# A hybrid decoder layer on one core: gate strips together, branch strips together, recurrent gates one tile later

## What is computed

```
xn = rmsnorm(x) * norm_mix
xl, gl, q, k, v, z, b, a, u_pool, g_lru, g_dn, g_pool = split(xn @ w_in)
o_lru  = rg_lru(conv4(xl)) * gelu(gl)          # gates: tanh of block-diagonal products of conv4(xl)
o_dn   = gated_delta_rule(silu(conv4(q,k,v)), b, a) ... * silu(z)
o_pool = multiscale causal pooling of u_pool
merged = sigmoid(g_lru)*(o_lru @ w_br_lru) + sigmoid(g_dn)*(o_dn @ w_br_dn) + sigmoid(g_pool)*(o_pool @ w_br_pool)
x = x + merged @ w_out
x = x + relu(rmsnorm(x) @ w_up)**2 @ w_down
y = rmsnorm(x) * norm_final
```

## Time and profile before

| what | value |
|---|---|
| time, median of 3 runs | 2197.82 us (2196.42 to 2201.01) |
| profiled execution, its own time | 2197.58 us |
| its span | 2195.8 us |
| PE busy (matmul) | 2157.2 us, 98% |
| DVE, ACT, POOL busy | 1223.4, 784.4, 176.0 us |
| DMA mean | 141 GB/s |

### The profile page before, as it was taken

One profiled execution on the slowest core, in us unless ns is written; L12 is line 12 of the kernel. 1 busy time (PEld: TensorE's weight loads), 2 busy tenths in 40 slices (PEclk: granted clock), 3 DMA queues, 4 the chain that ended last, 5 costly groups with the idle time before them and its releaser, 6 DMA issues.

```text
span 2195.8 us, 35754 instructions
## 1 busy us (share of the span) xinstructions
PE 2157.2 (98%) x14507; PEld 2096.5 (95%) x14507; DVE 1223.4 (56%) x1993; ACT 784.4 (36%) x946; POOL 176.0 (8%) x325
## 2 busy tenths in 40 slices
PE   8999998999999999999999999999999999999997
PEld 8998997899998899989999999999999999999997
DVE  7996786555566555555554554444444444444444
ACT  5434553222222222233333443333333333333243
POOL 7000011110022110010000100000000000000001
PEclk9999999999999999999999999999999999999998
DMA  6454444343354343346444444444444544444443
GB/s 216 140 158 135 130 126 132 107 121 113 96 171 125 107 122 109 96 136 197 149 146 153 151 143 149 150 153 146 152 148 150 153 146 149 153 148 153 145 144 106
DMA packets 295610, 308.96 MB, mean 141 GB/s; under 512 B 9713, under 2 KB 290417, under 8 KB 295233
## 3 DMA queue, kind: packets, MB, share of 16 engines
q1 hardware_dynamic: 291616, 291.54, 43.0%
q0 software_dynamic: 3584, 15.55, 2.4%
q10 hardware_dynamic: 288, 0.15, 0.0%
HBM read 298.83 MB, written 8.37 MB: 140 GB/s over the span
## 4 chain that ended last, share of the span: by engine, by line
PE 85%; DVE 8%; ACT 3%; issue 3%; POOL 1%; DMA 1%; DVEq 0%; ACTq 0%; SPq 0%; POOLq 0%
PE main L1420 26%; PE main L1421 25%; PE main L1422 25%; PE aux L1540 6%; DVE scratch L883 2%; DVE scratch L876 2%; DVE lo L876 1%; ACT hi L608 1%; DMA raw<-in_w_in 1%; DVE scratch L880 1%; PE aux L1523 0%; PE aux L1513 0%; POOL qkv L368 0%; DVE merged L876 0%; DVE scratch L879 0%
## 5 line engine op out<-in xcount | busy, mean ns | idle before, releaser
L876 DVE TENSOR_TENSOR lo<-raw,hi 128x1024 fp32r<-128x1024 f32 x546 | 670.0, 1235 | 571.6 <-ACT hi L608 565.4
L608 ACT ACTIVATE hi<-raw 128x1024 fp32r<-128x1024 f32 x546 | 573.4, 1056 | 934.8 <-PE main L1422 920.2
L1420 PE MATMUL main<-x_hi,hi 128*128 128x320 f32 x2688 | 842.8, 314 | 3.0 <-DVE x_lo L883 1.7
L1421 PE MATMUL main<-x_lo,hi 128*128 128x320 f32 x2688 | 831.6, 309 | 0.0
L1422 PE MATMUL main<-x_hi,lo 128*128 128x320 f32 x2688 | 831.5, 309 | 0.0
L1420 PEld LDWEIGHTS main<-x_hi,hi 128*128 128x128 f32 x2688 | 505.9, 188 | 10.5 <-issue 5.2
L1421 PEld LDWEIGHTS main<-x_lo,hi 128*128 128x128 f32 x2688 | 506.0, 188 | 0.8 <-issue 0.2
L1422 PEld LDWEIGHTS main<-x_hi,lo 128*128 128x128 f32 x2688 | 505.5, 188 | 0.0
L1420 PE MATMUL main<-o_hi,hi 128*128 128x320 f32 x1408 | 442.4, 314 | 4.6 <-DVE o_lo L876 4.6
L1421 PE MATMUL main<-o_lo,hi 128*128 128x320 f32 x1408 | 435.5, 309 | 0.0
L1422 PE MATMUL main<-o_hi,lo 128*128 128x320 f32 x1408 | 435.5, 309 | 0.0
(11 more groups left out here) (249 smaller groups left out, 1187.7 us busy)
## 6 DMA issues: line engine op xcount, KB each, us to landing
raw<-in_w_in SPq DMA_DIRECT2D x210, 512.0 KB, 3.7
raw<-in_w_up SPq DMA_DIRECT2D x128, 512.0 KB, 3.8
raw<-in_w_down SPq DMA_DIRECT2D x128, 512.0 KB, 3.4
raw<-in_w_back SPq DMA_DIRECT2D x80, 512.0 KB, 3.4
scratch<-in_s_in POOLq DMA_DIRECT2D x8, 512.0 KB, 4.7
out_s_out<-scratch POOLq DMA_DIRECT2D x8, 512.0 KB, 4.5
merged<-in_x SPq DMA_DIRECT2D x8, 320.0 KB, 7.7
qkv<-in_x POOLq DMA_DIRECT2D x1, 2560.0 KB, 10.4
```

The costliest lines, as they stand in the source:

```text
L608: act.activation(HI[:, slot * TILE:(slot + 1) * TILE], RAW[:, slot * TILE:(slot + 1) * TILE], ACT.Copy).then_inc(hi_ready, 1)
L876: return dve.tensor_tensor(out, a, b, op)
L1420: pe.matmul(bank, hi, xh, start=first, stop=False)
L1421: pe.matmul(bank, hi, xl, start=False, stop=False)
```

## The change

A gated iteration runs both gate strips (tiles 0 to 7), then both branch strips (tiles 8 to 11), with loads in the same new order. There are two gate buffers, `GATE = (GS, GS1)`. The memory of the second comes from `RN` and `BG`, which become halves of `GS`. On DVE `gate(1)` stands at position 12 (was: position 2 of the next iteration), `merge(0)` at position 2 of the next iteration (was: position 10), and ACT's tanh goes with the gate. The products `gates(it)` of the LRU pass, which stood at the end of tile 7, stand at the end of tile 0 of the next iteration, or of the first tile of `GPL`. PE's loop over the LRU iterations is unrolled. DVE's and ACT's orders in the LRU pass are as they were.

```diff
-        GS = sb("gate", 2 * N)
-        RN, BG = sb("qk_scale_rows", N), sb("beta_gamma_rows", N)
+        GS, GS1 = sb("gate", 2 * N), sb("gate_second", 2 * N)
+        GATE = (GS, GS1)
+        RN, BG = GS[:, 0:N], GS[:, N:2 * N]
...
             def gated(it, n0, name):
                 for s in range(2):
                     for j in range(4):
-                        load(n0, 12, it, 6 * s + j, A["w_in"], j * 512, it * 512 + (G0[name] + s * 256))
+                        load(n0, 12, it, 4 * s + j, A["w_in"], j * 512, it * 512 + (G0[name] + s * 256))
+                for s in range(2):
                     for j in range(2):
-                        load(n0, 12, it, 6 * s + 4 + j, A["w_back"], BACK[name] + j * 512, it * 512 + s * 256)
+                        load(n0, 12, it, 8 + 2 * s + j, A["w_back"], BACK[name] + j * 512, it * 512 + s * 256)
...
-                own = {8: [lambda: gate(it, 0, t0, 0)]}
+                own = {8: [lambda: gate(it, 0, t0, 0)], 12: [lambda: gate(it, 1, t0, 0)]}
...
             def gate(n0, t0, it, s):
-                tile_done(n0, 12, it, 6 * s + 3)
-                dve.wait_ge(evacuated, it * 8 + (t0 + 4 * s + RING))
-                for m in range(2):
-                    tt(GS[:, m * N:(m + 1) * N], MB[m][:, 0:N], R[:], ALU.mult).then_inc(evacuated, 1)
+                tile_done(n0, 12, it, 4 * s + 3)
+                dve.wait_ge(evacuated, it * 8 + (t0 + 2 * s + RING))
+                for m in range(2):
+                    tt(GATE[s][:, m * N:(m + 1) * N], MB[2 * s + m][:, 0:N], R[:], ALU.mult).then_inc(evacuated, 1)
...
-                own = {8: [lambda: gate(n0, t0, it, 0)], 10: [lambda: merge(n0, t0, g0, it, 0, branch)]}
+                own = {8: [lambda: gate(n0, t0, it, 0)], 12: [lambda: gate(n0, t0, it, 1)]}
...
-                steps = {2: [lambda: gate(n0, t0, it, 1)], 4: [lambda: merge(n0, t0, g0, it, 1, branch)]}
+                steps = {2: [lambda: merge(n0, t0, g0, it, 0, branch)], 4: [lambda: merge(n0, t0, g0, it, 1, branch)]}
...
-                    3: [(7, lambda: qk_sums(3))], 7: [(7, lambda: gates(0))]})
-            with pe.Fori(1, 4) as it:
-                lru(it, {7: [(7, lambda: gates(it))]})
+                    3: [(7, lambda: qk_sums(3))]})
+            for it in range(1, 4):
+                lru(it, {0: [(7, lambda it=it: gates(it - 1))]})
...
-                    strip(n0, 12, t0, 8, it, 6 * s, 4 * s, XH, XL, between=between)
-
-                    strip(n0, 12, t0, 8, it, 6 * s + 4, 4 * s + 2, OH, OL,
+                    strip(n0, 12, t0, 8, it, 4 * s, 2 * s, XH, XL, between=between)
+                for s in range(2):
+                    strip(n0, 12, t0, 8, it, 2 * s + 8, 2 * s + 4, OH, OL,
...
-            gated(0, GPL_N, GPL_T, 0, 4, 0)
+            gated(0, GPL_N, GPL_T, 0, 4, 0, {0: [(7, lambda: gates(3))]})
```

More of the change, by code:

```diff
@@ L727, in gate @@
             def gate(it, s, t0, g0):
-                act.wait_ge(evacuated, it * 8 + (t0 + 4 * s + 2 + RING))
-                act.activation(GS[:], GS[:], ACT.Tanh, scale=0.5).then_inc(gate_ready, 1)
+                act.wait_ge(evacuated, it * 8 + (t0 + 2 * s + 2 + RING))
+                act.activation(GATE[s][:], GATE[s][:], ACT.Tanh, scale=0.5).then_inc(gate_ready, 1)
             def dn_step(h, k):
@@ L766, in late @@
             def late(it, t0, h0):
-                steps = {2: [lambda: gate(it, 1, t0, 0)]}
-                return steps if h0 is None else joined(steps, dn_steps(dn_step, it + h0, False, True))
+                return dn_steps(dn_step, it + h0, False, True)
             gated(0, GPL_N, GPL_T, 0, lru_steps(lru_step, 3), True)
@@ L803, in gated_dn @@
                 walk(split, GPD_N, 12, it, 12, {**after, 8: [lambda: gate(it, 0, GPD_T, 0)],
-                                                10: [lambda: merged_hi(it * 2)]})
+                                                12: [lambda: gate(it, 1, GPD_T, 0)]})
             def late_dn(it):
-                return {2: [lambda: gate(it, 1, GPD_T, 0)], 4: [lambda: merged_hi(it * 2 + 1)]}
+                return {2: [lambda: merged_hi(it * 2)], 4: [lambda: merged_hi(it * 2 + 1)]}
             gated_dn(0, {4: [lambda: z_gate(3)]})
@@ L1055, in row_norms @@
                 dve.wait_ge(sq_used, 1 + 16)
-                link(rsqrt(2, AX[1][0:16, 0:N], ROW[4], ROW[5], ROW[6], RN[0:16, :], 1.0, SMALL[0:16, 0:1]))
+                link(rsqrt(2, AX[1][0:16, 0:N], ROW[4], ROW[5], ROW[6], RN[0:16], 1.0, SMALL[0:16, 0:1]))
                 rows_split(0, RN)
@@ L1121, in gate @@
             def gate(n0, t0, it, s):
-                tile_done(n0, 12, it, 6 * s + 3)
-                dve.wait_ge(evacuated, it * 8 + (t0 + 4 * s + RING))
+                tile_done(n0, 12, it, 4 * s + 3)
+                dve.wait_ge(evacuated, it * 8 + (t0 + 2 * s + RING))
                 for m in range(2):
-                    tt(GS[:, m * N:(m + 1) * N], MB[m][:, 0:N], R[:], ALU.mult).then_inc(evacuated, 1)
+                    tt(GATE[s][:, m * N:(m + 1) * N], MB[2 * s + m][:, 0:N], R[:], ALU.mult).then_inc(evacuated, 1)
             def merge(n0, t0, g0, it, s, branch):
-                tile_done(n0, 12, it, 6 * s + 5)
+                tile_done(n0, 12, it, 2 * s + 9)
                 dve.wait_ge(gate_ready, it * 2 + (g0 + s + 1))
                 for m in range(2):
-                    dst = GS[:, m * N:(m + 1) * N] if branch else cols(MG, it, 4 * N, (2 * s + m) * N, N)
-                    stt(dst, GS[:, m * N:(m + 1) * N], 1.0, MB[2 + m][:, 0:N], ALU.add, ALU.mult) \
+                    own = GATE[s][:, m * N:(m + 1) * N]
+                    dst = own if branch else cols(MG, it, 4 * N, (2 * s + m) * N, N)
+                    stt(dst, own, 1.0, MB[2 * s + m][:, 0:N], ALU.add, ALU.mult) \
                         .then_inc(evacuated, 1)
@@ L1136, in merge @@
                     return
-                dve.wait_ge(evacuated, it * 8 + (t0 + 4 * s + 4 + RING))
+                dve.wait_ge(evacuated, it * 8 + (t0 + 2 * s + 6 + RING))
                 sums = cols(MG, it, 4 * N, 2 * s * N, 2 * N)
-                ins = tt(sums, sums, GS[:], ALU.add)
+                ins = tt(sums, sums, GATE[s][:], ALU.add)
                 if branch == 1:
```

## The result

| | before | changed |
|---|---|---|
| median of the runs | 2198.4 us (4 runs, 2196.4 to 2201.0) | 2212.3 us (4 runs, 2210.9 to 2214.9) |
| ratio, 95% interval | | 1.0066 (1.0050 to 1.0082) |
| profiled execution, own time | 2197.6 us | 2212.4 us |
| its span | 2195.8 us | 2210.6 us |
| granted clock, mean | 0.994 | 0.992 |

The changed kernel is slower by some 14 us. PE's work is the same, as the page's line of busy time shows against the earlier trace rows: 3 us more on 14507 instructions, which is slow clock, since the instructions are the same.

What follows compares the result with a forecast made beforehand. PE is busy 98%, but the LRU pass was taken as bound by a closed chain through PE, ACT and DVE. 8.0 + 4.8 + 4.3 + 1.4 + 0.3 = +18.8 on 2197.6 gave 2216.4, as median 2216.6 us, range 2206 to 2224.

Steps and rivals of the forecast that it cites:

- The chain in the LRU pass: LRU pass: the convolution comes 2.65 us later in each of three periods, 34.5 instead of 31.9; +8.0 us.
- The head of `GPL`: Head of `GPL`: ACT's tanh, `o_ready` and the first head's step 0 come 4.8 us later, without cover; +4.8 us.
- The clock in front of step 0: Tile 0 in two looped LRU iterations and at `GPL`'s head: new PE waits lower the clock; +4.3 us.
- The clock behind step 0: Behind the first head's step 0 in `GPL`: clock low after PE's wait of 9 to 10 us; +1.4 us.
- The moved gates and merges: Gated passes: changed DVE orders, gains at merges against losses at the gate; +0.3 us, from -2.6 to +5.
- The scaling ahead of step 9: Position 12 in each of two passes: strip 1's gate delays the head's steps; +0.88 us each, +1.8.
- The merge that left the place ahead of step 1: First iteration of `GPL`: gain of up to 0.88 us, half usable, -0.4; in `GPP` -1.1.
- The looped iterations: Looped gated iterations: costed at nothing, covered by a half tile of 1.8 us; otherwise up to 0.9 each of six.
- the second buffer frees PE: Rival: gate products hide behind tile 0, PE's waits and a slow stretch go; -9.9, 2187.7 us; chance 7%.
- The balance: Rival: half the chain's growth hidden, clock stays up, losses met by a removed wait; about 2198 us; chance 4%.
- The case without the clock: Rival: the chain grows but the clock stays high; 13.1 us slower, 2211 us; chance 15%.
- The case where the clock costs more: Rival: a second slow stretch follows each slow tile 0, doubling both clock terms; 2222 us; chance 12%.

Runs made afterwards that it cites:

- e5: The changed kernel with DVE's convolution one position later, behind the split of the next tile 0 instead of ahead of it: 2199.7 us, ratio 1.0007.
- e3: The changed kernel with POOL's rows of the first head computed ahead of its wait for `o_ready`: 2207.9 us, ratio 1.0040.
- e4: e1 with POOL's rows of the first head computed ahead of its wait for `o_ready`: 2193.6 us, ratio 0.9982.
- e6: The changed kernel plus 16 unused matmuls at the end of tile 7 in the last three LRU iterations: 2208.8 us, ratio 1.0052.
- e2: The kernel before with only the gate products moved behind tile 0, gated passes and their one buffer kept: 2211.2 us, ratio 1.0059.
- e1: The kernel before with only the new gated order and two gate buffers, gate products still at tile 7: 2196.8 us, ratio 0.9995.
- e10: e4 with gate strip 1's scaling and tanh moved into the next iteration, and three ACT splits ahead of LRU steps in `GPL`: 2189.8 us.
- e8: e1 with the scaling of gate strip 1 behind the head's steps of position 12: 2202.8 us, ratio 1.0023.

## Why the prediction was right, and where it was off

The forecast was 2216.6 us and the median 2212.3: the direction, the mechanism and the place are right, and the size is 4.3 us too large. The measured terms below are from the profiled execution, +14.8 against a forecast of +18.8. They add up to +15.0; in this trace PE is already 0.25 us earlier before the first moved product, which is the two executions' own.

**The chain in the LRU pass: +8.0 forecast, +7.2 measured.** The period at full clock is 34.3 instead of 31.9 to 32.0, 2.4 for 2.65. The cover was taken as 2.05 us, the two waits of ACT, and came out as 2.2 to 2.3; the row at 275.26, where no idle time is left, fits that. That PE would stand 3.9 us at tile 0 was wrong in form: it stands 2.40 there and 1.15 at tile 4, for banks. I had written that nothing behind the two waits of ACT depends on PE, and had not looked the other way, at what PE takes back from the recurrence. In the changed kernel it costs nothing, as PE has slack; in e5 it became the bound.

**The head of `GPL`: +4.8 forecast, +4.7 measured.** `o_ready` came at 367.15, 30.6 us behind the convolution's end, against 24.5 before: 6.1, of which 1.4 are tile 0's slow clock, counted below. Step 0 moved with it and POOL's rows remained the last to end; e3 and e4 show that by taking them away. PE waited 8.6 us there and not 9 to 10: it reached the place 25.4 us behind the convolution instead of 24, in part by a wait of 0.80 at tile 4.

**The clock in front of step 0: +4.3 forecast, 4.3 measured** (two slow tiles in the periods at 1.5, one ahead of `o_ready` at 1.4); taking the sum from e6 instead gives 3.5 in the medians. The mechanism is shown by e6. That all three tiles were slow, as forecast, is luck of the profiled execution: e2's and e3's traces have the same waits and one slow tile each.

**The clock behind step 0: +1.4 forecast, +2.0 measured** (16.0 at step 0, 18.0 at tile 6). Step 0's own matmuls took 1.43 instead of the 0.86 of the earlier trace rows, which I had not counted.

**The moved gates and merges: +0.3 forecast, -3.2 measured.** This is the mis-sized term. Of the 3.5 us between the two, 1.45 are no effect of the change but the clock of the two profiled executions, and some 2 us are. Its parts, from the counted tiles:

- The scaling ahead of step 9: +0.8 in each of the two peeled iterations, as forecast (0.88), and the wait at step 10 is 1.11 instead of the 0.32 of the earlier trace rows.
- The merge that left the place ahead of step 1: -0.7 in `GPL` for -0.4. In `GPP` the wait at step 2 fell from 2.85 to 1.74, the 1.1 that was forecast; but this trace also lacks a slow stretch that the trace of before has right behind that wait (granted 0.50 from 695.7 to 699.1), 0.8 us more. In e2, which keeps the old order, that stretch is missing too, at 0.75. So it is not an effect of the order. The wait in `GPP`, in the trace of before and of the changed kernel:

```profile
693.84 0.61 PE L1566 MATMUL aux<-ident,scratch 128*128 128x128 f32 x3 [2.85 <-DVE scratch L876]
```

```profile
710.54 0.61 PE L1568 MATMUL aux<-ident,scratch 128*128 128x128 f32 x3 [1.74 <-DVE scratch L877]
```

- The looped iterations, costed at nothing: -0.1 each in `GPL`, -0.4 each in `GPP`, -1.45 together. e1 has the same numbers, e2 none. The step that failed is the cover: I held half a tile between two steps on PE to be enough room for 0.9 us on DVE, without reading any looped iteration's row.
- The last stretch of the span: -0.65. It is there in e1 and e4 and not in e5 and e10, and no edit touches it. It is the clock again: in front of the last six products PE waits 1.67 us in both traces, and then they took 1.54 us before, at a granted 0.50, and 0.88 us in the changed kernel, at 1.00. Before and changed:

```profile
2184.86 1.54 PE L1726 MATMUL aux<-ident,scratch 128*128 128x128 f32 x6 [1.67 <-DVE scratch L876]
```

```profile
2200.32 0.88 PE L1728 MATMUL aux<-ident,scratch 128*128 128x128 f32 x6 [1.67 <-DVE scratch L877]
```

The medians cannot show the 2 us either: e1, which has these moves alone, is 0.8 us below before, with an interval from 3.1 less to 0.9 more.

**The rivals.** That the second buffer frees PE is refuted. In the changed kernel both waits that it counted on went, and came back as waits for splits, banks and rows; in e1, with the buffer and the order alone, the 4.6 us for `o_lo` came back as 6.1 for the rows. The balance is refuted with it, since e2 alone carries the loss. The case without the clock, priced at 2211 us, lies near the median, but for another reason: the clock term is real, as e6 shows by taking 3.5 us away, while the chain and the moved gates and merges came out lower than forecast. The case where the clock costs more, 2222 us, did not come: behind each slow tile 0 PE ran at full clock again, and the stretch of 10.3 us around step 0 cost 2.0.

## What to carry to other kernels

Before work is moved on the bound engine, look for the loop that closes once per iteration through the other engines, and add up its period: if it is longer than the bound engine's work, whatever is put between two of its links is paid, however early it frees that engine, less the time that the other engines stood idle for it (here 4.7 us were put in and 2.4 paid). Then look for the second loop, which decides what a repair of the first can bring: here the release of banks went through the same recurrence, and 31.9 could only become 31.7. And when an instruction is moved, find out which engine waits for it in order: e8 lost 6 us by moving the half of a pair.

## What the runs showed of the hardware

The clock's answer to the same wait was not the same each time. A wait of 2.4 us at tile 0 was followed by a slow stretch three times of three in the changed kernel's trace (granted 0.53 from 266.0 to 269.5, 0.72 from 301.9 to 305.3, 0.54 from 337.8 to 341.2), and once of three in e2's and in e3's. In e2 the second such wait, of 2.40 us, was followed by this row:

```profile
301.90:305.30 3.40, 3.36 (x23) 3.36 (x24) 2.25 (x2) 0.00 (x0) 0.00 (x0) 1.00 0.62 172
```

So the price of a wait of this length is anything from nothing to some 1.5 us, and a forecast can only bound it. The 1.67 us in front of the last products had both answers too. Waits of 0.78 to 1.15 us in the LRU pass were followed by full clock every time in the changed kernel's and e2's traces, and those of 1.31 to 1.33 us in before's and e1's. Around the wait of 8.6 us the stretch at 1.2 GHz in the changed kernel's trace lasted 10.3 us. PE was busy for 4.52 of them, and the place of tile 6 shows that this cost 2 us.

For the low-clock price the Trainium skill, "TensorE: Matmul & The Clock Gate", section Terms, has the slow stretch's time multiplied by what is missing of the clock. For a slow tile 0 of 3.4 us at 0.50 that would be an estimate of 1.7 us; the periods here show 1.5, so the trace agrees to 0.2.
